# One encoder layer on one core: the third branch's group norm and the second gate's sums change places on VectorE

## The reference, cut to what matters

```python
h = rmsnorm(x, norm_mix);  proj = h @ w_in          # also holds the three gates
y_a = rglru_branch(...) @ w_a_proj
y_b = sgu_branch(...)   @ w_b_proj
y_c = ssd_branch(...)   @ w_c_proj
g = sigmoid(gates)                                   # 3 gates of width 1024
merged = g[0] * y_a + g[1] * y_b + g[2] * y_c
x = x + merged @ w_out
x = x + cross_attention(rmsnorm(x), rmsnorm(mem))    # 4 heads, 256 memory tokens
x = x + hierarchical_moe(rmsnorm(x))                 # 32 experts, 2 per token
out = rmsnorm(x)

# the end of ssd_branch, the third branch's group norm:
yg = (y * silu(z)).reshape(bsz, s, 4, 256)           # 4 groups of 256 columns
return rmsnorm(yg, norm_g.reshape(4, 256))
```

## Time and profile before

| | us |
|---|---|
| median of 3 runs | 1011.41 (1008.98 to 1012.88) |
| the profiled execution | 1014.7 |
| its span, first to last instruction | 1012.8 |
| busy in the span: PE, POOL, DVE, ACT | 859.3, 211.1, 293.3, 192.3 |

### The profile page before, as it was taken

The page is one execution under the profiler, slowest core; times in us unless marked ns, Lnnn a source line. Parts: engine busy times, 40 slices in busy tenths (PEclk is TensorE's granted clock), DMA queues, the critical chain, the costliest instruction groups (busy, mean ns, idle before and its releaser), DMA issues.

```text
span 1012.8 us, 17255 instructions
## 1 busy us (share of the span) xinstructions
PE 859.3 (85%) x7608; PEld 647.0 (64%) x7608; DVE 293.3 (29%) x785; ACT 192.3 (19%) x354; POOL 211.1 (21%) x120
## 2 busy tenths in 40 slices
PE   8999999999995999999999899676765776566575
PEld 7888866888995999999668565333333333233332
DVE  2344101646135443342210544212211211221212
ACT  1322126851122100010210221111011111101102
POOL 1000000003996787997001000000000000000000
PEclk9899999999997999999999999977888878988987
DMA  9544434442452444444894699999999999999994
GB/s 298 159 166 166 161 131 158 133 167 83 167 208 83 167 167 167 167 166 167 341 406 166 251 426 426 426 429 425 428 426 426 428 427 427 426 427 428 426 427 192
DMA packets 62400, 285.24 MB, mean 282 GB/s; under 512 B 6693, under 2 KB 11641, under 8 KB 50169
## 3 DMA queue, kind: packets, MB, share of 16 engines
q1 hardware_dynamic: 52736, 278.96, 68.9%
q10 hardware_dynamic: 9592, 5.19, 1.9%
HBM read 283.08 MB, written 1.06 MB: 281 GB/s over the span
## 4 chain that ended last, share of the span: by engine, by line
PE 62%; DMA 25%; SPq 5%; DVE 3%; another core or an unknown queue 2%; POOL 1%; issue 1%; ACT 0%; ACTq 0%; DVEq 0%; POOLq 0%
PE bank L1639 20%; PE bank L1468 20%; DMA ring<-in_w_gate_up_dram 10%; PE bank L1480 5%; SPq L398 5%; PE bank L1822 5%; DMA ring<-in_w_down_dram 5%; DMA params<-in_w_gate_up_dram 5%; DMA blk<-in_w_down_dram 5%; PE bank L1844 3%; PE bank L1541 1%; PE bank L1791 1%; PE bank L1783 1%; PE bank L1715 1%; PE bank L1695 1%
## 5 line engine op out<-in xcount | busy, mean ns | idle before, releaser
L1468 PE MATMUL bank<-blk,ring 128*128 128x256 f32 x896 | 198.9, 383 | 0.8 <-DVE blk L1237 0.8
L1468 PEld LDWEIGHTS bank<-blk,ring 128*128 128x128 f32 x896 | 170.6, 192 | 25.6 <-issue 1.4
L1639 PE MATMUL bank<-ring 128*128 128x128 f32 x1088 | 127.8, 276 | 0.4 <-POOL ring L507 0.4
L1639 PEld LDWEIGHTS bank<-ring 128*128 128x128 f32 x1088 | 124.9, 193 | 0.7 <-issue 0.6
L1822 PE MATMUL bank<-ring,cbm 128*32 128x256 f32 x1088 | 80.0, 443 | 38.6 <-DMA ring<-in_w_gate_up_dram 38.6
L1639 PE MATMUL bank<-blk,ring 128*128 128x128 f32 x816 | 98.5, 278 | 10.7 <-DVE blk L1162 10.5
L1639 PEld LDWEIGHTS bank<-blk,ring 128*128 128x128 f32 x816 | 95.7, 195 | 11.6 <-issue 11.5
L480 POOL TENSOR_TENSOR ring<-ring 128x1024 f32<-128x1024 f32 x17 | 40.0, 2353 | 259.9 <-PE bank L1601 235.9
L1822 PE MATMUL bank<-blk,cbm 128*32 128x256 f32 x768 | 58.9, 458 | 34.9 <-DMA blk<-in_w_gate_up_dram 34.7
L1326 DVE TENSOR_TENSOR cbm<-bank,gq 128x256 f32<-128x256 f32 x32 | 13.6, 425 | 250.9 <-PE bank L1791 250.9
L1822 PEld LDWEIGHTS bank<-ring,cbm 128*32 128x32 f32 x1088 | 39.3, 123 | 72.8 <-issue 54.1
(11 more groups left out here) (307 smaller groups left out, 881.5 us busy)
## 6 DMA issues: line engine op xcount, KB each, us to landing
ring<-in_w_gate_up_dram SPq DMA_DIRECT2D x34, 2048.0 KB, 49.7
blk<-in_w_gate_up_dram SPq DMA_DIRECT2D x24, 2048.0 KB, 50.2
ring<-in_w_in_dram SPq DMA_DIRECT2D x19, 2048.0 KB, 7.8
ring<-in_w_down_dram SPq DMA_DIRECT2D x18, 2048.0 KB, 49.9
blk<-in_w_down_dram SPq DMA_DIRECT2D x10, 2048.0 KB, 49.5
params<-in_w_gate_up_dram SPq DMA_DIRECT2D x6, 2048.0 KB, 50.0
ring<-in_w_kv_dram SPq DMA_DIRECT2D x4, 2048.0 KB, 8.0
params<-in_w_down_dram SPq DMA_DIRECT2D x3, 2048.0 KB, 50.9
```

Source lines behind the costliest of these rows:

```text
L1468: last = mm(ps[:, f * T:(f + 1) * T], w[:, k, c:c + P], src[:, k, :], start=k == 0, stop=k == KD - 1)
L1639: last = mm(ps[:, f * P:(f + 1) * P], wt[:, k, f * P:(f + 1) * P], xt[:, k, :], start=k == 0, stop=k == 3)
```

## The change

On DVE the call `fold("gB", 0, gateT, 0)` moves from ahead of the group norm to behind it. Nothing is added, removed or resized, and the other engines' instructions stay in their order.

```diff
             merge("A", 1)
-            fold("gB", 0, gateT, 0)
 
             def crms_bank(g):
                 return bank(f"cn{g // 2}")[:, g % 2 * T:(g % 2 + 1) * T]
...
                                               in1=crms_bank(f * GROUPS // KD), op0=ALU.mult, op1=ALU.mult)
                 if f % 4 == 3:
                     last.then_inc(read["cn"], 1)
+            fold("gB", 0, gateT, 0)
             merge("B", 0)
             fold("gB", 1, gateT, 4)
```

## The result

| | before | after |
|---|---|---|
| median of the runs | 1010.64 us (4 runs, 1008.98 to 1012.88) | 996.57 us (4 runs, 994.55 to 998.03) |
| the profiled execution | 1014.7 us | 994.55 us |
| its span | 1012.8 us | 992.8 us |

The ratio is 0.9861, with a 95% interval of 0.984 to 0.9881: 14 us less, between 12 and 16. The forecast was 12.7 less, at 998.7; it started from the 1011.41 us that were known then, and the median of before is 0.8 lower here. The two profiled spans differ by 20.0 us, more than the medians, so where the profiles differ has to be sorted before it is put down to the change.

A forecast was written before the change was run, and what follows sets the result against it. The prediction took PE as the bound, with one hole waiting for the norm: 10.5 us of pause plus 2.25 of low clock make 12.75, and 1011.4 - 12.7 = 998.7 us. Range 996 to 1003, 8 in 10.

The forecast's parts named there:

- The bound, and the pause: Between gB0 and pB0, PE waits 10.5 us for the norm's last scaling to release the cn banks; that hole goes.
- The clock: At pB0's start, PE's clock is low after idling; without the pause pB0 takes 12.51 us, not 14.76, giving 2.25.
- The sum at its place: At gB1's start, 10.5 + 2.25 = 12.75 us gained: PE starts gB1 at 318.2 in place of 330.94.
- The norm's cover: Beside gB0, the norm ends at about 303.9, 1.8 us before PE wants pB0's banks at 305.67.
- No stretch: The norm keeps its 9.93 us beside PE's matmuls; bad end half as much again, with PE waiting 3.1 us.
- The fold, late: Fold gB0 starts at 303.9, not 300.40, and ends at 306.6; cost nothing, the nearest waiter having 1.8 us to spare.
- POOL: Its operations for pB0 stay ahead of PE by 1.8, 1.2, 0.7 and 1.8 us, L490 tightest; no stall.
- the rival of a disturbance between the two: Norm and POOL slow each other at 293.9 to 303.9 us: time 1010 if POOL stood still; chance 0.06.
- To the end: In the experts' stage, loads are started by PE, so the weight stream comes 12.75 us earlier with the same length.
- Rival 2: In the experts' stage, the gain is given back to a weight stream whose start does not move: 1011.4; chance 0.04.
- Rival 3: TensorE's clock falls to 1.2 GHz in the longer busy run, 11.6 us more per half; 1021.9 with two; chance 0.03.
- the stated range: Whole time 996 to 1003 us, from norm stretch (+3.1), clock share (+2.25) and about 2 us scatter; 8 in 10.

The follow-up runs named there:

- e5: Kernel before with VectorE's order untouched, PE beginning pB0's third and fourth banks only ahead of the products that write them; ratio 0.9894, 10.7 us less.
- e4: Kernel before with only the two reciprocals moved ahead of fold gB0, the eight scalings left behind it; ratio 0.9925, 7.6 us less.
- e9: Kernel before with 45 idle matmuls put in PE's pause ahead of pB0; ratio 0.9945, 5.6 us less.
- e6: Changed kernel with one more reciprocal (3.38 us) in front of the norm; ratio 0.9905 against the kernel before.
- e11: Changed kernel with two more reciprocals (6.7 us) between the norm's last scaling and fold gB0; 996.7 us, ratio 0.9855 against the kernel before.
- e10: Changed kernel with 57 idle matmuls in front of pB0; 1009.94 us, ratio 0.9994 against the kernel before.
- e12: Changed kernel with ten idle matmuls where PE waits for the router's assignment; 996.29 us, ratio 0.9852 against the kernel before.
- e1: Changed kernel run again, unaltered, beside the kernel before; 996.34 against 1009.85 us, ratio 0.9873.
- e8: Kernel before profiled again, one execution, for its stage lengths; 290.46 us to gB0, 280.97 to the first expert matmul, 439.1 to the end.
- e2: Kernel before with 90 idle matmuls in front of pB0, 20.3 us, overrunning the pause by 9.4; ratio 1.011.
- e3: Changed kernel with 115 idle matmuls (25.7 us) in front of pB0; 1023.26 us, ratio 1.0131 against the kernel before.
- e7: Changed kernel with two more reciprocals (6.75 us) in front of the norm; ratio 0.9927 against the kernel before.

## Why the prediction was right

*The bound, and the pause.* Right. PE's only long wait was the release of the `cn` banks; e5 removes most of it from PE's side, e4 a part from VectorE's. Measured from start to start the pause was 10.7 us, not 10.5: I took the time at which PE's last matmul ended, but in an unbroken row the next product starts 1.79 us after the last one's start, so 0.2 before that end. The last product of gB0 in the kernel before started at 303.70, so pB0 could have started at 305.49:

```profile
303.70 1.95 PE L1639 MATMUL bank<-ring 128*128 128x128 f32 x16
```

*The clock.* Right: 2.25 predicted, 2.18 in e9, where nothing but PE's idleness was taken away.

*The sum at its place.* 12.75 predicted, 12.95 measured.

*The norm's cover.* 1.8 us predicted, 1.4 measured: in e6 3.4 us more of norm cost 2.0 at its place. In the changed kernel 300.53 - 298.96 = 1.6 lie between the two, of which PE takes some 0.14 to start once the banks are free (in e6 the last scaling ends at 304.58 and pB0 starts at 304.72). Most of the rest is the 0.2 us by which PE wants the banks earlier. No stretch, as predicted: the reciprocals beside PE's writes to other banks take 6.76 us, with PE idle 6.75.

*The fold, late.* Right, and safer than I said: it ended at 301.54, and e11 adds 6.7 us at no cost.

*POOL.* Right. L490 took 2.36 beside PE's work and ended at 305.48; pB0's fourth product wanted it at 300.53 + 5.37 = 305.90. So 0.4 us were left of the 0.7. Its combos beside the norm took 1.27 to 1.29 us, without it 1.26 to 1.27; the rival of a disturbance between the two falls. The trace agrees with the letter of the rule of the Trainium skill that the prediction weighed (GPSIMD Engine Reference, Key points: contention when VectorE runs a two-port mode or has two SBUF inputs): each instruction of the norm reads one large tensor from SBUF, and neither engine's instructions grew by more than 0.03 us.

*To the end.* Rival 2 falls by e10 and by SP's issues. The experts' stage does wait for its weights, PE for 121.5 us in the kernel before and 125.9 after. But the first expert load (L398) is issued 153.9 us after gB1's start in both and in e10 (at 484.86, 466.95 and 480.26), so the whole stream moved with PE, as predicted. Rival 3 falls by the clock of 1.00 from 300.5 to 540.

*What the forecast lacked.* In the profiles 15.0 us are gained behind the start of gB0, 2.1 more than the shift. The median of 996.57 lies only 0.6 us above the lower end of the stated range, 996; the sum had no term for a gain behind the attention, and the terms that the prediction names for its range give 998.7 - 2 = 996.7 as the lower end. That the range held is to that extent luck. Part of the extra gain can be seen. Here is the stretch of the kernel before just ahead of the first expert, and one of the kernel after, with the granted clock (the third number from the end):

```profile
570.00:573.00 3.00, 2.84 (x17) 1.18 (x18) 1.74 (x8) 0.05 (x1) 0.00 (x0) 0.50 0.00 0
```
```profile
543.50:546.50 3.00, 3.00 (x19) 3.00 (x19) 2.17 (x14) 2.02 (x4) 0.00 (x0) 0.63 1.01 431
```

Around the router PE has little work, and in both kernels the clock falls once. In the kernel before it fell after PE's wait of 2.8 us for the assignment, on the path: the gather of 16 instructions took 1.93 us. In the kernel after it fell earlier, over the transposes (3.00 us in place of 1.95), which PE had time for, since it then waited only 1.1 us, and the gather took 1.07:

```profile
570.16 1.93 PE L1791 MATMUL bank<-blk,dec 128*32 128x256 f32 x16 [0.49 <-DVE dec L1311]
```
```profile
543.55 3.00 PE L1754 MATMUL bank<-ident,blk 128*128 128x128 f32 x16
...
552.25 1.07 PE L1791 MATMUL bank<-blk,dec 128*32 128x256 f32 x16 [0.49 <-DVE dec L1311]
```

That is the 1.2 us of the third stage. e12 bears it out: with the clock kept up all through, the stage is 11.1 too, so an early fall costs nothing and a late one does. Over the fourteen profiles the stage is 11.1 in six (after, e1, e5, e9, e11, e12) and 12.2 to 13.0 in eight (before, e8, e2, e3, e4, e6, e7, e10). It does not belong to VectorE's order: e5 and e9 have the old order and 11.1, e3, e6, e7 and e10 the new and 12.4 to 12.95. What places the fall is open, and so are the 0.9 us of the experts' stage, which runs from 437.8 to 440.7 over the profiles without a pattern that I can name. The timed runs point the same way without settling it: e12's gain of 13.5 to 16.3 us and e9's of 4.0 to 7.1 lie wholly above their shifts (12.95 and 2.2), e2's loss lies above its own, and the intervals of the others, some 1.5 to 2.5 us to each side, hold theirs. So 13.0 us of the gain are shown to be the change; the 1 to 2 beyond it are shown only to be there, and another edit at this place may lose them.

## What to carry to other kernels

When an engine that takes its instructions in order releases a scarce buffer, look at what stands in its line ahead of the release: here 10 us of ready work stood behind sums that could not run before PE had finished. Move the release to where its input is ready, check the next supplier's lead (here 0.4 us was left), and add what the clock costs after the pause. A buffer ring fed by an ordered list also hides such a wait in a place that has no data in common with it; taking banks one by one, when they are written, gets most of the gain without touching the order.

## What the runs showed of the hardware

The price of the clock's fall grew far less than the pause: behind a pause of 3.9 us pB0 took 1.7 us longer than the 12.51 of a half at full clock (e4), behind 5.4 us 1.8 (e7), behind 10.7 us 2.25 and 2.4 (before, e8), and behind 2.0 us 0.07 (e6). Each is one trace. And the clock also fell with PE shown as fully busy: 0.63 in the stretch from 543.5 of the kernel after, behind the router's matmuls of one and 36 columns. The kernel before ran the same matmuls and kept 1.00 over its transposes, so they alone do not place the fall. A float32 matmul of the program is two instructions in the trace, 0.112 us each for 128 columns at full clock.
